# First mixer of a two-part transformer: chunk order, head grouping and attention placed among the weight chunks

## The chip, the core and the metric

The kernel runs as one program on one core of a Trainium2 chip. The metric is device microseconds for one execution, the median of several runs. TensorE (PE) multiplies matrices out of SBUF into the eight banks of PSUM; VectorE (DVE), ScalarE (ACT) and GpSimd (POOL) do the elementwise work; SyncE (SP) issues the weight loads.

## The reference

A sequence of 256 tokens with 1024 features passes through two two-layer models, all in f32. The order is: first mixer ("even"), convolutional feed-forward, forgetting attention ("fox"), convolutional feed-forward, gated feed-forward, recurrent mixer ("hgrn"), gated feed-forward, shared keys and values ("kv"), gated feed-forward, dilated attention, gated feed-forward. Each block works on a root-mean-square norm of the residual x and adds to it. Cut to the first mixer:

```
sq, sk, sv, nq, kc, vc, ksl, vsl, kwn, vwn, g = split_cols(h @ w_in, EVEN_SPLITS)
o_sb  = stick_breaking_attention(heads(sq), heads(sk), heads(sv))     # 8 heads of 64
o_nsa = nsa_attention(partial_rope(nq), kc, vc, partial_rope(ksl), vsl,
                      partial_rope(kwn), vwn, sigmoid(g), pos_k, pos_v, w_ck, w_cv)
return concat(o_sb, o_nsa) @ w_out
# stick breaking: z = q k / 8; log_keep = masked log_sigmoid(-z)
#   a = masked exp(log_sigmoid(z) + sum of log_keep over later keys);  o = a v
# nsa: kc, vc = windows of 32 tokens (every 16, 15 windows) + position, times w_ck, w_cv;
#   o = g0 * softmax over the 15 compressed + g1 * softmax over selected + g2 * softmax over window
```

With 256 tokens all selected blocks and the whole window are causal attention over everything, so the last two branches are ordinary causal softmaxes with their own keys and values: 8 heads x 2 branches, done as 8 units of two heads (4 pairs x 2 branches).

## The kernel before

x lies with features on partitions, as 8 tiles of 128 x 256. Before each block ScalarE writes xh, the f32r part of x times the gain (line 991), and VectorE writes xl, the remainder (line 891), by pairs of tiles; `act_prep` and `dve_prep` do this, with the squares for the norm, which is applied to results later. Weights come in chunks of 256 columns (1 MB) into a ring of three slots. ScalarE makes the high part of a chunk (line 342, `hi`) and VectorE or GpSimd the remainder (line 348, `lo`; the list `lo_by` says which). A product is three matmuls (lines 375 to 377), high by high, low by high, high by low; a chunk of both halves has 16 products of 256 columns, 48 matmuls. `chunk_mul` counts finished chunks: it frees a ring slot for the next high part, and `lo_ok` starts the next load. Each engine follows an order written out by hand; all coupling is by semaphores.

`make_even` holds the first mixer. TensorE (`pe_part`) takes chunks 0 to 11 in the order of the columns: queries and keys of the stick-breaking heads (0 to 3), their values (4, 5), queries of the other heads (6, 7), compressed keys and values (8), selected and windowed keys and values (9, 10, each with an extra half, 72 matmuls), gates (11, 24 columns). Only then come: the two position transposes, the compression (lines 1127 and 1132, 128 small matmuls) out of blocks that VectorE builds (line 1238); ten rotations (lines 1159, 1161) with VectorE's cosine and sine work (1251 to 1255); stick breaking for eight heads, namely scores (1145, 1146), suffix sums (1170 to 1174), values (1180, 1182), between them ScalarE's absolute value, exponential and logarithm (1326 to 1334) and VectorE's factors and masks (1259 to 1265); the compressed scores (1190), their softmax on VectorE and transposes (1197). Then the softmax stage (`Soft`, `soft_pe`, `soft_dve`, `soft_act`): scores (438), mask (531), maxima (536, 537), exponentials (604), reciprocals and gates (549, 551), weights (555), transposes (456 to 458), values (472 to 478), two rounds late. Last the four output chunks (`pe_residual`), whose activations are kept in xh and xl themselves, so that the next block's xh waits for the last chunk (`outputs_in_xh`).

The forgetting mixer uses the same softmax stage, but its chunks stand among the units by the hooks `before`, `mid`, `after` and `step`, and its outputs lie in `dk_r`.

## Time and profile before

| | us |
|---|---|
| median of 3 runs | 2120.63 (2119.83 to 2125.02) |
| profiled execution | 2131.83 |
| its span | 2130.0 |
| TensorE busy | 2002.0 (94%) |
| VectorE busy | 1239.2 (58%) |
| ScalarE busy | 993.7 (47%) |
| mean granted TensorE clock | 0.959 |

In the page's forty slices of 53 us, TensorE is at 9 or more in nearly all; the third and fourth slices have 8 and 7 busy tenths and a granted clock of 5 and 7 tenths. The chain that ended last lies to 79% on TensorE. Idle time counts only where it is on the engine that sets the end; the granted clock says how long a matmul takes while it is busy.

### The profile page before, as it was taken

What the parts mean: (1) busy time and instruction counts of PE and PEld (TensorE: products, weight loads), DVE (VectorE), ACT (ScalarE), POOL (GpSimd) and SP (SyncE); (2) the same over time, 40 slices, a digit from 0 to 9 for tenths busy, and PEclk for the clock granted to TensorE, in tenths of its full rate; (3) what the DMA queues carried; (4) which work ended last, traced back from release to release, by engine and by line L of the source; (5) the groups of instructions that cost most, each with busy time, mean ns of one, the idle gap of its engine ahead of it and who ended that gap; (6) DMA issues with size and microseconds to landing.
All of it is one profiled execution on the core that took longest, in us unless ns stands there. A gap on an engine that the chain in (4) does not pass through costs nothing.

```text
span 2130.0 us, 36855 instructions
## 1 busy us (share of the span) xinstructions
PE 2002.0 (94%) x15868; PEld 1913.7 (90%) x15868; DVE 1239.2 (58%) x1422; ACT 993.7 (47%) x1159; POOL 181.2 (9%) x74
## 2 busy tenths in 40 slices
PE   7887999999999989999886999999999998989999
PEld 7875899989899989999886999999899997769998
DVE  5327476675676676557785655543455565546554
ACT  4225444454544454346433533476743446655333
POOL 0100000001000000000341000033200010230000
PEclk9857899999999999999988999999999999999999
DMA  7300354444255435554321455545455545425552
GB/s 285 134 7 1 104 178 177 159 178 140 100 186 188 179 138 178 180 188 165 130 80 41 171 183 177 178 155 170 158 178 179 186 150 189 126 80 178 178 179 98
DMA packets 57569, 321.13 MB, mean 151 GB/s; under 512 B 5949, under 2 KB 19380, under 8 KB 20084
## 3 DMA queue, kind: packets, MB, share of 16 engines
q1 hardware_dynamic: 55700, 313.93, 42.6%
q10 hardware_dynamic: 1760, 5.63, 0.7%
q8 instruction: 84, 1.38, 0.3%
q14 instruction: 25, 0.20, 0.0%
HBM read 318.41 MB, written 1.12 MB: 150 GB/s over the span
## 4 chain that ended last, share of the span: by engine, by line
PE 79%; DVE 12%; ACT 5%; issue 2%; DMA 1%; SPq 0%; POOL 0%; ACTq 0%; DVEq 0%
PE bank L375 24%; PE bank L377 23%; PE bank L376 23%; DVE lo L348 3%; ACT hi L342 1%; DVE xl L891 1%; PE bank L438 1%; PE bank L475 1%; PE bank L1583 1%; DVE arena L531 1%; ACT arena L1744 1%; DVE arena L1658 1%; PE bank L1127 1%; PE bank L1132 1%; DVE x L904 1%
## 5 line engine op out<-in xcount | busy, mean ns | idle before, releaser
L375 PE MATMUL bank<-xh,hi 128*128 128x256 f32 x3080 | 885.1, 287 | 30.1 <-DVE xl L891 20.4
L376 PE MATMUL bank<-xl,hi 128*128 128x256 f32 x3080 | 878.3, 285 | 0.0
L377 PE MATMUL bank<-xh,lo 128*128 128x256 f32 x3080 | 877.9, 285 | 0.0
L348 DVE TENSOR_TENSOR lo<-ring,hi 128x2048 fp32r<-128x2048 f32 (+1 forms) x269 | 632.8, 2356 | 314.5 <-ACT hi L342 313.9
L342 ACT ACTIVATE hi<-ring 128x2048 fp32r<-128x2048 f32 x291 | 552.4, 1900 | 493.2 <-PE bank L377 486.3
L375 PEld LDWEIGHTS bank<-xh,hi 128*128 128x128 f32 x3080 | 597.5, 194 | 44.9 <-issue 31.2
L376 PEld LDWEIGHTS bank<-xl,hi 128*128 128x128 f32 x3080 | 597.6, 194 | 0.6 <-issue 0.5
L377 PEld LDWEIGHTS bank<-xh,lo 128*128 128x128 f32 x3080 | 597.4, 194 | 0.2
L375 PE MATMUL bank<-gh,hi 128*128 128x256 f32 x1056 | 300.1, 284 | 7.2 <-DVE gl L821 7.2
L376 PE MATMUL bank<-gl,hi 128*128 128x256 f32 x1056 | 299.4, 284 | 0.0
L377 PE MATMUL bank<-gh,lo 128*128 128x256 f32 x1056 | 299.3, 283 | 0.0
L375 PEld LDWEIGHTS bank<-gh,hi 128*128 128x128 f32 x1056 | 203.3, 193 | 8.2 <-DVE gl L821 8.2
L376 PEld LDWEIGHTS bank<-gl,hi 128*128 128x128 f32 x1056 | 203.4, 193 | 0.0
L377 PEld LDWEIGHTS bank<-gh,lo 128*128 128x128 f32 x1056 | 203.3, 193 | 0.0
L348 POOL TENSOR_TENSOR lo<-ring,hi 128x2048 fp32r<-128x2048 f32 (+1 forms) x22 | 97.7, 4439 | 1055.4 <-ACT hi L342 1055.4
L375 PE MATMUL bank<-hi,xh 128*128 128x256 f32 (+1 forms) x400 | 119.8, 300 | 0.9 <-DVE arena L1398 0.8
L376 PE MATMUL bank<-lo,xh 128*128 128x256 f32 (+1 forms) x400 | 114.5, 286 | 0.0
L377 PE MATMUL bank<-hi,xl 128*128 128x256 f32 (+1 forms) x400 | 114.4, 286 | 0.0
L852 ACT ACTIVATE gh<-arena 128x512 fp32r<-128x512 f32 x66 | 41.7, 632 | 126.1 <-DVE arena L818 126.1
L790 DVE TENSOR_TENSOR arena<-bank,rs_b 128x512 f32<-128x512 f32 x66 | 45.6, 691 | 94.0 <-PE bank L377 93.8
L531 DVE TENSOR_TENSOR arena<-bank,arena 128x384 f32<-128x384 f32 x80 | 40.8, 552 | 75.0 <-PE bank L458 35.9
L375 PEld LDWEIGHTS bank<-hi,xh 128*128 128x128 f32 x400 | 78.6, 197 | 4.2 <-issue 2.8
(268 smaller groups left out, 2002.8 us busy)
## 6 DMA issues: line engine op xcount, KB each, us to landing
ring<-in_ffn_in SPq DMA_DIRECT2D x132, 1024.0 KB, 4.9
ring<-in_ffn_out SPq DMA_DIRECT2D x66, 1024.0 KB, 4.9
ring<-in_kv SPq DMA_DIRECT2D x24, 1024.0 KB, 4.9
ring<-in_hg_in SPq DMA_DIRECT2D x16, 1024.0 KB, 4.9
ring<-in_od_in SPq DMA_DIRECT2D x12, 1024.0 KB, 5.0
ring<-in_dq SPq DMA_DIRECT2D x12, 1024.0 KB, 4.9
ring<-in_ev_in SPq DMA_DIRECT2D x11, 1024.0 KB, 5.7
arena<-rel_rows SPq DMA_DIRECT2D x24, 256.0 KB, 3.8
```

The costliest lines, as they stand in the source:

```text
L342: nc.scalar.activation(hi[n % RING][:, 0:words[n]], ring[n % RING][:, 0:words[n]], ACT.Copy).then_inc(hi_ok, 1)
L348: ns.tensor_tensor(lo[n % RING][:, 0:w], ring[n % RING][:, 0:w], hi[n % RING][:, 0:w].bitcast(F32), ALU.subtract).then_inc(lo_ok[lo_by[n]], 1)
L375: nc.tensor.matmul(out_, lh, rh, start=start, stop=False, **kw)
L376: nc.tensor.matmul(out_, lh, rl, start=False, stop=False, **kw)
L377: return nc.tensor.matmul(out_, ll, rh, start=False, stop=stop, **kw)
L438: last = nc.tensor.matmul(soft_bank(w, e)[:, c0:c1], sub["q"][:, q0:q0 + P], sub["k"][:, 0:k1], start=True, stop=one)
L475: nc.tensor.matmul(out[e][:, 0:T], un["subs"][e][g]["v"][0], s.pt[w % 2][e][:, 0:T], start=un["first"] and g == 0, stop=False, skip_group_ ...
L531: nc.vector.tensor_tensor(a[e][:, g, :], soft_bank(w, e)[:, 0:384], un["subs"][e][g]["add"], ALU.add).then_inc(soft_sem["masked"], 1)
L790: nc.vector.tensor_tensor(dst, ga, rs2, ALU.mult).then_inc(ff_read, 1)
L852: nc.scalar.activation(gh[:, par, :, :], ff_g[:, par, :, :], ACT.Copy).then_inc(gh_ok, 1)
L891: last = nc.vector.scalar_tensor_tensor(xl[:, t, :], x[:, t, :], gain_of(b, t), xh[:, t, :].bitcast(F32), ALU.mult, ALU.subtract)
L904: nc.vector.scalar_tensor_tensor(xs, y, scale, xs, ALU.mult, ALU.add).then_inc(x_new, 1)
```

## The change

- The first mixer's chunks come in the order stick-breaking queries, keys and values of the first four heads (0, 2, 4 of before), compressed keys and values (8), selected and windowed keys (9), their values (10), the other queries (6, 7), the gates, and then queries, keys and values of the last four stick-breaking heads (1, 3, 5). The columns of the weights are regrouped beforehand, so that keys of both branches share a chunk, as do the values, and no chunk has an extra half. The other heads are paired (0,4), (1,5), (2,6), (3,7), so that each pair's two heads belong to the two groups; the duplicating constants are gone.
- Stick breaking runs in two groups of four heads: the first among chunks 3 to 6, the second behind the softmax stage, among the output chunks.
- Rotation is applied to a raw copy of a whole chunk, 512 columns at once, three times; norm and scale are folded into the cosine and sine.
- Compression is one run of 32 matmuls with keys and values merged in the weights (128 columns) against blocks filled up with zeros.
- The softmax stage has six half chunks (9, 10, 11, all in bank 3) among its first six rounds, the compressed softmax spread over rounds 0 to 4, and the output chunks go by tiles in the order 0, 1, 4, 5, 6, 7, 2, 3.
- All remainders of the first mixer are made by VectorE.
- Outputs of the first mixer lie in `dk_r`. After "hgrn" and "kv" the last chunk's second half frees xh by pairs of tiles (`xh_free`), where the whole chunk was awaited.

```diff
-            "even": [cols("ev_in", CW * c) for c in range(11)] + [cols("ev_in", 2816, 24)]
+            "even": [cols("ev_in", CW * c) for c in (0, 2, 4, 8, 9, 10, 6, 7)] + [cols("ev_in", 2816, 24)]
+            + [cols("ev_in", CW * c) for c in (1, 3, 5)]
...
-            elif b == "hgrn":
+            elif b in ("even", "hgrn"):
...
+                if freed and h == 1 and k in (1, 3, 5):
+                    last.then_inc(xh_free, 1)
...
+                if i == 2 and outputs_in_xh(r):
+                    for t in range(3):
+                        low(t)
...
-            return r["kind"] == "add" and r["y"][0][0] == "c" and r["after"] not in ("fox", "dilated")
+            return r["kind"] == "add" and r["y"][0][0] == "c" and r["after"] not in ("even", "fox", "dilated")
...
+            by_tiles = r["kind"] == "regain" or outputs_in_xh(r)
+            if info[b]["c0"] > 0 and not by_tiles:
+                act.wait_ge(chunk_mul, info[b]["c0"] - 2)
             if b == plan[0]:
                 hi_until(act, 0)
             for i in range(4):
                 if r["kind"] != "regain":
                     act.wait_ge(x_new, r["x0"] + i + 1)
+                if by_tiles:
+                    act.wait_ge(*((xh_free, r["free0"] + i + 1) if i < 3 else (chunk_mul, info[b]["c0"])))
                 for e in range(2):
...
+            def sb_bank(grp, i):
+                return bank[4 * (1 - grp) + i]
...
+            rope_chunk, rot_bank = (4, 6, 7), (5, 4, 5)
+            rope_dst = (KD[:, :, :], NQ[:, 0:2, :], NQ[:, 2:4, :])
+            rope_scale = (1.0, DH ** -0.5, DH ** -0.5)
...
+            def pe_rot(pe, r):
+                pe.wait_ge(raw_ok, r + 1)
+                nc.tensor.matmul(bank[rot_bank[r]][:, :], C["rot"][:, :], RAW[:, r % 2, :, :], start=True,
+                                 stop=True).then_inc(rot_mm, 1)
...
+            def dve_cos(dve, r):
+                dve.wait_ge(raw_ok, r + 1)
+                nc.vector.scalar_tensor_tensor(rope_dst[r], halves(bank[rope_chunk[r] % 4]), rope_scale[r], two(COSR[:, :]),
+                                               ALU.mult, ALU.mult).then_inc(cos_ok, 1)
...
+            def dve_rope(dve, r):
+                dve.wait_ge(rot_mm, r + 1)
+                if r >= 1:
+                    dve.wait_ge(rope, r)
+                nc.vector.scalar_tensor_tensor(RT[:, :, :], halves(bank[rot_bank[r]]), rope_scale[r], two(SINR[:, :]),
+                                               ALU.mult, ALU.mult).then_inc(rope_t, 1)
+                dve.wait_ge(rope_t, r + 1)
+                dve.wait_ge(cos_ok, r + 1)
...
+            def pe_compress(pe):
+                pe.wait_ge(cmp_in, 16 * 2)
+                pe.wait_ge(blk_ok, 8)
+                for l in range(32):
+                    last = nc.tensor.matmul(bank[7][:, 0:64], CW_[:, l, :], BLOCKS[:, l, :], start=l == 0, stop=l == 31)
+                last.then_inc(comp, 1)
...
+            def out_part(pe, c, ks):
+                for h in range(2):
+                    if h == 0 and 0 in ks and c >= 2:
+                        pe.wait_ge(*soft.at("o", c + 1))
+                    pe_part_of(pe, n0 + 12 + c, bank[4 + c], h, ks, lambda k: pe.wait_ge(*of_tile(k)), (out_h, out_l),
+                               tile_order)
...
+            def pe_round_half(c, h):
+                def run(pe):
+                    if (c, h) == (9, 0):
+                        pe.wait_ge(cos_ok, 3)
+                    elif h == 0:
+                        pe.wait_ge(pj_fm, c - 6)
+                    pe_half(pe, n0 + c, bank[3], "tm" if c == 11 else "fm", h)
+                    if (c, h) == (9, 0):
+                        pe_cmp_scores(pe)
+                return run
...
+            soft.before["pe"] = {0: pe_first, 8: pe_last_scores}
+            soft.after["pe"] = {2: pe_turn_two, 3: pe_turn_third, 4: pe_turn_fourth}
+            soft.turn_after = {1: (c_pt, 2), 3: (c_pt, 4)}
...
+            soft.before["dve"] = {1: lambda dve: lo_until(dve, n0 + 11), 2: lambda dve: dve_evict(dve, 9),
+                                  4: lambda dve: dve_evict(dve, 10)}
+            soft.mid["dve"] = {0: dve_first}
+            soft.after["dve"] = {1: dve_cmp_weights, 3: lambda dve: lo_until(dve, n0 + 12),
+                                 5: lambda dve: lo_until(dve, n0 + 13), 7: lambda dve: lo_until(dve, n0 + 14)}
+            soft.tail["dve"] = {7: lambda dve: sb_keep(dve, 1)}
...
+            soft.mid["act"] = {1: act_cmp_exps, 3: act_pairs_turned, 4: lambda act: act_cmp_turned(act, 2),
+                               5: lambda act: act_cmp_turned(act, 3)}
+            soft.after["act"] = {2: lambda act: hi_until(act, n0 + 12), 4: lambda act: hi_until(act, n0 + 13),
+                                 6: act_last_values, 8: lambda act: sb_abs(act, 1), 9: lambda act: sb_logs(act, 1)}
...
+            def pe_part(pe):
+                pe_chunk(pe, n0, bank[0], "fm", first=first_xg("even"))
+                pe_stats(pe, "even")
+                pe_chunk(pe, n0 + 1, bank[1], "fm")
+                pe_chunk(pe, n0 + 2, bank[2], "tm")
+                pe.wait_ge(pos_in, 16 * 2)
+                nc.tensor.transpose(bank[6][:, 0:64], PE_[0:64, :], ident[0:64, 0:64]).then_inc(pos_t, 1)
+                pe.wait_ge(pj_fm, 2)
+                pe.wait_ge(pos_ok, 1)
+                sb_scores(pe, 0)
+                pe_chunk(pe, n0 + 3, bank[3], "fm")
+                pe.wait_ge(pj_fm, 1)
+                pe_chunk(pe, n0 + 4, bank[0], "fm")
+                pe.wait_ge(const_in, 16)
+                pe.wait_ge(ones_ok, 2)
+                sb_suffix(pe, 0)
+                pe.wait_ge(pj_fm, 2)
+                pe_chunk(pe, n0 + 5, bank[1], "tm")
+                pe.wait_ge(pj_tm, 1)
+                sb_values(pe, 0)
+                pe_rot(pe, 0)
+                pe_chunk(pe, n0 + 6, bank[2], "fm")
+                pe_compress(pe)
+                pe.wait_ge(pj_fm, 3)
+                pe_chunk(pe, n0 + 7, bank[3], "fm")
+                pe_compressed_keys(pe)
+                pe_rot(pe, 1)
+                pe.wait_ge(cos_ok, 1)
+                pe_chunk(pe, n0 + 8, bank[0], "tm", 24)
+                pe.wait_ge(rope, 1)
+                pe_rot(pe, 2)
+                soft_pe(pe, soft)
+                out_part(pe, 0, (0, 1, 4, 5))
+                out_part(pe, 1, (0, 1, 4, 5))
+                sb_suffix(pe, 1)
+                out_part(pe, 0, (6,))
+                out_part(pe, 1, (6,))
+                out_part(pe, 2, (0, 1, 4, 5))
+                sb_values(pe, 1)
+                for c in range(2):
+                    out_part(pe, c, (7,))
+                out_part(pe, 2, (6, 7))
+                for c in range(3):
+                    out_part(pe, c, (2, 3))
+                for h in range(2):
+                    pe_half(pe, n0 + 15, bank[7], "fm", h, acts=(out_h, out_l))
...
+            def dve_ahead(dve):
+                nc.vector.memset(BLOCKS[:, :, :], 0.0).then_inc(ones_ok, 1)
+                nc.vector.memset(ONES[:, :], 1.0).then_inc(ones_ok, 1)
...
+            def dve_part(dve):
+                lo_until(dve, n0 + 3)
+                dve_evict(dve, 0)
+                dve_evict(dve, 1)
+                lo_until(dve, n0 + 4)
+                dve.wait_ge(pos_t, 1)
+                nc.vector.tensor_copy(PEK[:, :, :], bank[6][:, 0:64].rearrange("p (i l) -> p i l", i=2)).then_inc(pos_ok, 1)
+                lo_until(dve, n0 + 5)
+                dve.wait_ge(const_in, 16)
+                for dst, n in ((COSR, "cos"), (SINR, "sin")):
+                    nc.vector.tensor_tensor(dst[:, :], C[n], rs_b[:, :], ALU.mult).then_inc(cs_ok, 1)
+                sb_keep(dve, 0)
+                dve_evict(dve, 3)
+                lo_until(dve, n0 + 6)
+                dve.wait_ge(cs_ok, 2)
+                dve_cos(dve, 0)
+                dve.wait_ge(ones_ok, 2)
+                dve.wait_ge(pos_ok, 1)
+                dve.wait_ge(pj_fm, 3)
+                sb_mask(dve, 0)
+                for i in range(2):
+                    for g in range(2):
+                        r = slice(g * DH, (g + 1) * DH)
+                        kv = KCV[r, i, :].rearrange("p (c l) -> p l c", l=16)
+                        for hf in range(2):
+                            pos = PEK[r, i, 16 * hf:16 * hf + 16].unsqueeze(2).broadcast_to([DH, 16, N_CMP])
+                            nc.vector.tensor_tensor(BLK[r, 16 * hf:16 * hf + 16, i, g, 0:N_CMP], kv[:, :, hf:hf + N_CMP], pos,
+                                                    ALU.add).then_inc(blk_ok, 1)
+                lo_until(dve, n0 + 7)
+                dve_rope(dve, 0)
+                sb_low(dve, 0)
+                lo_until(dve, n0 + 9)
+                dve_cos(dve, 1)
+                dve.wait_ge(comp, 1)
+                nc.vector.tensor_copy(KVR[:, :], bank[7][:, 0:64]).then_inc(kvr_ok, 1)
+                dve_cos(dve, 2)
+                dve_compressed_keys(dve)
+                dve_rope(dve, 1)
+                lo_until(dve, n0 + 10)
+                dve.wait_ge(pj_tm, 3)
                 soft_dve(dve, soft)
+                sb_mask(dve, 1)
+                sb_low(dve, 1)
+                lo_until(dve, n0 + 15)
...
             def act_part(act):
+                for i in range(2):
+                    act.dma_start(PE_[32 * i:32 * i + 32, :], A["cmp_pos"][:, i * P:(i + 1) * P]).then_inc(pos_in, 16)
...
+                act_evict(act, 2)
+                hi_until(act, n0 + 5)
+                sb_abs(act, 0)
+                sb_logs(act, 0)
+                hi_until(act, n0 + 6)
+                act_raw(act, 0)
+                hi_until(act, n0 + 7)
+                sb_exps(act, 0)
+                act_evict(act, 5)
+                hi_until(act, n0 + 8)
+                sb_high(act, 0)
+                act_raw(act, 1)
+                hi_until(act, n0 + 9)
+                act_raw(act, 2)
+                hi_until(act, n0 + 10)
+                act_evict(act, 8)
+                hi_until(act, n0 + 11)
                 soft_act(act, soft)
-            return {"pe": pe_part, "dve": dve_part, "act": act_part}
+                sb_exps(act, 1)
+                sb_high(act, 1)
+            return {"pe": pe_part, "dve": dve_part, "act": act_part, "dve_ahead": dve_ahead}
```

## Rows read from the trace of the kernel before

**Rows 1.** Stretches: length, busy (x) of PE, PEld, DVE, ACT, POOL; PEclk, DMA share, GB/s.
```profile
17.90:96.50 78.60, 78.59 (x631) 78.42 (x631) 34.38 (x31) 30.98 (x30) 9.85 (x3) 0.99 0.56 206
96.50:222.60 126.10, 99.55 (x642) 77.67 (x641) 61.94 (x177) 46.40 (x120) 4.56 (x1) 0.62 0.05 17
445.00:576.00 131.00, 126.85 (x1012) 114.10 (x1010) 76.63 (x139) 72.45 (x138) 18.67 (x4) 1.00 0.38 132
```

**Rows 2.** Waits between 96 and 223 us; columns: total, times, longest.
```profile
PE bank L1127 <- DVE arena L1238: 6.5, 1, 6.5
...
PE bank L1170 <- DVE arena L1262: 5.7, 1, 5.7
```

**Rows 3.** Busy time by stretch, pieces of the attention, columns as in rows 1.
```profile
103.50:130.40 26.90, 26.74 (x256) 26.44 (x256) 0.07 (x1) 0.00 (x0) 0.00 (x0) 0.50 0.12 40
151.20:154.30 3.10, 3.06 (x16) 2.68 (x16) 0.00 (x0) 1.03 (x3) 0.00 (x0) 0.50 0.00 0
164.50:168.90 4.40, 4.40 (x32) 4.13 (x30) 4.30 (x10) 1.01 (x3) 0.00 (x0) 1.00 0.00 0
169.00:172.60 3.60, 3.58 (x33) 2.52 (x32) 2.74 (x7) 3.48 (x9) 0.00 (x0) 1.00 0.00 0
```

**Rows 4.** Timeline of TensorE at three edges; columns: start, duration, instruction, idle before.
```profile
249.02 0.55 PE L375 MATMUL bank<-xh,hi 128*128 128x256 f32 x1 [2.01 <-DVE xl L891]
...
577.28 0.39 PE L375 MATMUL bank<-xh,hi 128*128 128x256 f32 x1 [0.96 <-DVE xl L891]
...
1538.33 0.35 PE L375 MATMUL bank<-xh,hi 128*128 128x256 f32 x1 [3.12 <-DVE xl L891]
```

**Rows 5.** Timeline of VectorE and ScalarE during the output chunks.
```profile
235.54 0.69 DVE L904 SCALAR_TENSOR_TENSOR x<-bank,x 128x512 f32<-128x512 f32 x1 [1.46 <-PE bank L377]
...
241.30 0.69 DVE L904 SCALAR_TENSOR_TENSOR x<-bank,x 128x512 f32<-128x512 f32 x1 [1.46 <-PE bank L377]
243.31 2.29 DVE L348 TENSOR_TENSOR lo<-ring,hi 128x2048 fp32r<-128x2048 f32 x1 [1.31 <-ACT hi L342]
...
241.36 1.92 ACT L342 ACTIVATE hi<-ring 128x2048 fp32r<-128x2048 f32 x1 [3.84 <-PE bank L377]
```

**Rows 6.** Timeline of TensorE, one softmax unit.
```profile
198.32 0.92 PE L438 MATMUL bank<-arena 64*128 64x256 f32 x8
...
200.26 0.65 PE L472 MATMUL bank<-arena 15*64 15x256 f32 x4
200.84 0.65 PE L475 MATMUL bank<-arena 128*64 128x256 f32 x4
...
201.64 0.49 PE L438 MATMUL bank<-arena 64*128 64x256 f32 x2
```

**Rows 7.** Groups of instructions by shape, VectorE; columns: busy, mean ns, idle before.
```profile
L1238 DVE TENSOR_TENSOR arena<-arena 128x240 f32<-128x240 f32 x4 | 6.2, 1610 | 0.0
```

**Rows 8.** Busy time by stretch, compressed softmax and softmax stage, columns as in rows 1.
```profile
173.50:185.00 11.50, 5.57 (x48) 4.11 (x48) 3.19 (x11) 2.21 (x5) 0.00 (x0) 0.67 0.00 0
185.00:199.00 14.00, 11.29 (x60) 8.22 (x60) 11.59 (x40) 8.79 (x34) 0.00 (x0) 0.54 0.00 1
199.00:213.00 14.00, 11.50 (x94) 6.92 (x90) 13.76 (x49) 10.96 (x41) 0.00 (x0) 1.00 0.00 1
```

**Rows 9.** Timeline of VectorE, one softmax round.
```profile
199.64 1.01 DVE L531 TENSOR_TENSOR arena<-bank,arena 128x384 f32<-128x384 f32 x2
...
201.61 0.17 DVE L549 RECIPROCAL arena<-arena 128x4 f32<-128x4 f32 x1
...
203.43 0.55 DVE L531 TENSOR_TENSOR arena<-bank,arena 128x384 f32<-128x384 f32 x1
```

**Rows 10.** Timeline of ScalarE, logarithms of the stick-breaking heads.
```profile
156.55 1.28 ACT L1334 ACT_TABLE_LOAD   x1
157.84 3.41 ACT L1334 ACTIVATE arena<-arena,one_c 128x768 f32<-128x768 f32 x4
```

**Rows 11.** Timeline of ScalarE after keys and values.
```profile
1536.37 2.89 ACT L991 ACTIVATE xh<-x,vecs 128x256 fp32r<-128x256 f32 x7
```

More of the change, by code:

```diff
@@ L662, in pe_stats, with pe_half @@
                                  stop=True).then_inc(fin_stat, 1)
-        def pe_half(pe, n, B, mode, h, width=CW, first=None, tiles=None, acts=None):
+        def pe_half(pe, n, B, mode, h, width=CW, first=None, tiles=None, acts=None, freed=False):
             if h == 0:
@@ L1193, in pe_part, with pe_cmp_turn @@
                 last.then_inc(c_qk, 1)
-                pe.wait_ge(c_p, 1)
-                for h in range(8):
+            def pe_cmp_turn(pe, p, B):
+                for e in range(2):
                     for t in range(2):
-                        last = nc.tensor.transpose(bank[h // 2][0:N_CMP, (h % 2) * T + t * P:(h % 2) * T + (t + 1) * P],
-                                                   CP[:, 8 * (h % 2) + 2 * (h // 2) + t, 0:N_CMP], ident[:, :])
+                        last = nc.tensor.transpose(B[0:N_CMP, e * T + t * P:e * T + (t + 1) * P],
+                                                   CP[:, 8 * e + 2 * p + t, 0:N_CMP], ident[:, :])
@@ new lines, in act_evict @@
+            def act_evict(act, c):
+                act.wait_ge(chunk_mul, n0 + c + 1)
+                B = bank[c % 4 if c < 9 else 3]
+                for t in range(2):
+                    y, r = B[:, t * CW:(t + 1) * CW], rs_c[:, t:t + 1]
+                    if c == 8:
+                        last = nc.scalar.activation(GT[:, t, :], y[:, 0:24], ACT.Sigmoid, scale=r)
+                    elif c == 5:
+                        last = nc.scalar.activation(VSW[:, :, t, :], y.rearrange("p (b d) -> p b d", b=2), ACT.Copy, scale=r)
+                    else:
+                        v = SV[:, t, 0:CW] if c == 2 else SV[:, t, CW:2 * CW]
+                        last = nc.scalar.activation(v, y, ACT.Copy, scale=r)
+                last.then_inc(pj_tm, 1)
```

501 lines of the change are left out of this document (233 added, 268 removed).

## The prediction

> **What bounds the kernel now.** I read the busy time and clock by stretches first, one to a block. TensorE is busy nearly all of every feed-forward block, so the place to look is the first mixer: its twelve input chunks are dense, and then come 126.1 us with 99.6 us busy at a mean granted clock of 0.62, which lies near the lower level (1.2 of 2.4 GHz) [rows 1]. The forgetting mixer, which weaves its attention between its chunks, fills 126.9 of 131.0 us at clock 1.00 [rows 1]. Next the waits in the bad stretch: TensorE waits 6.5 us for the compression's blocks, 5.7 us for the stick-breaking factors, and less for smaller things [rows 2]; that is too little to explain it. The cost is mostly work issued alone at half clock: compression alone is 26.9 us at 0.50 [rows 3]. So before, TensorE runs from 17.9 to 247.0 (the next block's first product starts at 249.02 after 2.01 idle [rows 4]): 229.1 us, all of it on the path that sets the end.
>
> **The dense work that is left.** Price everything on TensorE at the upper level.
> Input chunks: 78.6 us before [rows 1], the slow first one included. Chunks 9 and 10 lose a third of their 72 products each (the half computed in both orders). A chunk of 48 products takes 5.76, from 241.30 minus 235.54, when two of them were taken up [rows 5], so this is 48 x 0.12 = 5.8 less. Taking 78.4 up to the last product: 72.6.
> Stick-breaking: scores of 4 heads took 3.1 at clock 0.50 [rows 3], so 1.55 at the upper level, twice: 3.1. Suffix products of five heads 4.4 at 1.00, 0.88 a head: 7.0 for 8. Value products of 8 heads 3.6 [rows 3].
> Rotation: 16 products of 256 columns become 3 of 512; a 512-column head of the suffix takes 0.88: 2.6.
> Compression: 128 small products become 32 with 128 weight columns and 64 moving columns. The old row gives 26.9/128 = 0.21 at half clock [rows 3]. Below: half of that, 0.105 x 32 = 3.4. Above: each full-width weight load costs as much as a product of a chunk (0.12) and an f32 product appears as two instructions (256 for the old 128), so 0.24 x 32 = 7.7. I take 7.5, since the wider weights are new and the chunk row has just that width.
> Compressed keys 1.0 (six small products; 0 to 2); compressed scores 2.0 (16 of the small kind, 0.12 each); 16 transposes at (200.26 - 198.32 - 0.92)/6 = 0.17 each [rows 6], 2.7; positions 0.3.
> Eight softmax units: one with compressed values takes 201.64 - 198.32 = 3.32; without them 0.58 less [rows 6]: 4 x 3.32 + 4 x 2.74 = 24.2.
> Output: four chunks 23.0 and 0.3 for opening three banks.
> Sum: 72.6 + 3.1 + 7.0 + 3.6 + 2.6 + 7.5 + 1.0 + 2.0 + 2.7 + 0.3 + 24.2 + 23.3 = 149.9. Without any stall the block would end at 167.8.
>
> **Where it will still stall.** I walked the three instruction orders against each other.
> TensorE's row of work, with the durations above: chunks 0 to 2 until 38.6, scores, chunks 3 and 4, suffix products until 56.0, chunk 5 until 61.8, values and first rotation, chunk 6 until 70.2, compression, chunk 7, keys, second rotation, chunk 8 until 92.3, third rotation, and round 0 of the softmax stage from about 93. Until chunk 6 each wait is covered by a chunk. Eight block additions replace four, on half the partitions but with the same 240 elements each. The old ones take 1.61 us [rows 7]; below, half of it if only partitions counted; I take the full price, 12.9 us. VectorE reaches them at about 58.8, after the last stick-breaking mask, and ends at 71.7, where chunk 6 ends at 70.2: 1.5 us stall. Chunk 7's remainder is queued behind them, but compression covers it.
> The softmax stage may start when ScalarE has the gates of chunk 8: 0.7, with a table load ahead of it. In round 0 the compressed scores wait for the third rotation, which VectorE does after the first masks: 0.7.
> The largest one is round 2. Chunks 9, 10 and 11 share one bank, so chunk 10 waits for VectorE's eviction of chunk 9, and on VectorE ahead of it stand: the first part of the compressed softmax 1.4 (all of it is 3.2 busy, some 3.5 with gaps [rows 8]), the remainder of chunk 11 2.29 [rows 5], the masks of unit 1 (201.61 - 199.64 = 2.0), the weights of unit 0 (203.43 - 201.61 less 0.4 for a pair's low part: 1.4 to 1.5) [rows 9], the other part of the compressed softmax 2.1, the eviction 0.7. Starting at 99.5 that gives 109.5; TensorE is there at 105.3: 4.2 stall. Everything behind chunk 10 on TensorE, the first transposes too, is queued behind this wait. Chunk 11: 0.3.
> From round 6 no chunk is left to fill. VectorE needs 3.5 a round and 2.3 for a remainder in every second, TensorE 3.0: stalls of 0.3 in round 7 and 1.4 in round 9. The second stick-breaking group: ScalarE starts its exponential at 147.4 (1.48, a table load of 1.28, then logarithms of 0.9 each [rows 10]), VectorE's factors end at 155.4, while the first two output chunks cover TensorE to 154.6 and the suffix products to 158.1: nothing.
> Chunk 15 takes the ring slot of chunk 12, which is now finished almost last, at 168.5; its high and low parts take 1.9 + 2.3 [rows 5] and the hand-over: 172.8, where TensorE would be at 171.4: 1.4 stall. Waits for the transposed positions at the start: 0.6.
> Together 11.1: the block ends at 179.0 instead of 247.0, 68 us less. I take off 2 for a lower clock in rounds 7 to 9 and 2 for hand-overs between engines that a walk on paper leaves out.
> Side costs I set to nothing: the clearing of the blocks stands before VectorE's first copy, while it waits for the load of the vectors (bounds 0 to 1). The remainders that GpSimd made go to VectorE, counted above. ScalarE gets three more table loads of 1.28 [rows 10], 3.8 us in all. Their cover is the waits for chunks; without it 1.3 each is on the path, at most in the gates and in the second group.
> On those loads the Trainium skill (ScalarE: Activation LUTs, Table sets: the hidden batching unit) gives some 2.7 us a load; the trace has 1.28 and decides, by the page the second group would come 1.4 later, and be covered too.
>
> **The edges between blocks.** First mixer to feed-forward: outputs no longer lie in the normed input, so this edge becomes like the one after the forgetting mixer, 0.96 instead of 2.01 [rows 4], with a small second wait behind it: 0.6. Recurrent mixer: pairs 0 to 2 are ready early, but the third low part now stands ahead of the last residual on VectorE, and the last pair waits 1.4 behind the start: 0.5 gained (bounds -0.5 to 2.0). Shared keys and values to the next block: 3.12 idle [rows 4], and freeing by pairs buys nothing, since ScalarE starts the normed input at 1536.37 with no idle time before it [rows 11], 1.2 after the last product, straight behind other work of its own, and so is itself late (bounds 0 to 2). Together 1.1.
>
> **The sum.** 68 - 2 - 2 + 1.1 = 65 us off. The profiled execution took 2131.8 us (span 2130.0), 11.2 above the median of 2120.6; the gain is taken as the same in both: 2067 profiled, 2056 for the median.
>
> **Rivals.**
> *Denser than I think.* If VectorE's pieces overlap as in the woven mixer, and chunk 10 doesn't wait, the block ends at 167.8: 79 + 1 off, 2040. For it: the forgetting mixer idles only 4 of 131 us [rows 1]. Against: it has twelve chunks to put between eight units, this one three.
> *The attention pieces keep the lower clock.* The unwoven softmax ran at 0.54 in one stretch and at 1.00 in the next [rows 8]. Were rounds 6 to 9 and the compression at the lower level, this costs 12 - 4 = 8 (rounds of which 4 is hidden in VectorE's time) and 7.5: 15 more, 2071. Against: a chunk half stands next to most pieces. The Trainium skill (TensorE: Matmul & The Clock Gate, Part 4: PE-mode transpose) says that transposes don't count as activity for the clock in the same way, which speaks for this case; the stretch at 1.00 held transposes in every round, which speaks against.
> *Slower than before.* One mechanism: the short gaps after chunk 2 drop the clock and the mixed work never brings it back until the block ends. Of the dense work 149.9 - 20.7 = 129 us comes later than chunk 2; at half clock it costs 129 more, 2185. It is slower than before from the point where 65 of these 129 us run at the lower level. In the stretch before, 126 us averaged 0.62, so it isn't impossible; the woven mixer's 1.00 speaks against.
> *It doesn't do what it says* holds for the keys-and-values edge, where I expect no gain; it is in the sum.
>
> **How the numbers follow.** Forecast 0.51, denser 0.17, lower clock 0.28, slower 0.04. The forecast alone spans 2046 to 2066 (each stall from nothing to double). The range 2040 to 2079 takes in most of both neighbours, the compression's lower price and the late ScalarE. Under 0.3%, 6.4 us, can't be told from no change; between the cases that fall there I put 0.01. Faster 0.95, same 0.01, slower 0.04.
>
> **What would show it.** The output chunks' last product near 182, not 247; compression as one run of some 7.5 us; clock at 0.95 or more from chunk 2 to the outputs; an idle gap of some 4 us ahead of chunk 10 released by VectorE's eviction; VectorE's 1.61 us additions eight times; the idle before the block after keys and values still near 3.1. I am wrong if TensorE waits on VectorE in most rounds, if the clock sits at 0.5 in the softmax stage, or if the end comes from another block.

## The result and the profile after

| us | before | after |
|---|---|---|
| median, same rounds | 2122.82 (2119.83 to 2130.67, 4 runs) | 2067.28 (2065.64 to 2069.61, 4 runs) |
| profiled execution | 2131.83 | 2066.73 |
| its span | 2130.0 | 2064.9 |
| mean granted clock | 0.959 | 0.979 |

The ratio is 0.9734, 95% interval 0.9704 to 0.9763: faster. The profiled executions lie 65.1 us apart, as forecast (65); the medians lie 55.5 apart, so the forecast of the median, 2056, is 11 too low.

Where it went, by stretches of the profile after (length, busy of PE, PEld, DVE, ACT, POOL, then PEclk, DMA share, GB/s):

```profile
16.90:82.00 65.10, 64.66 (x525) 62.60 (x526) 41.41 (x54) 33.77 (x40) 0.00 (x0) 1.00 0.54 196
82.00:95.00 13.00, 13.00 (x64) 10.86 (x63) 4.96 (x10) 6.22 (x6) 0.00 (x0) 0.61 0.24 82
95.00:109.40 14.40, 9.27 (x95) 8.46 (x93) 11.99 (x33) 4.13 (x17) 0.00 (x0) 0.97 0.22 73
109.40:115.00 5.60, 5.60 (x26) 5.60 (x27) 3.33 (x12) 0.00 (x0) 0.00 (x0) 0.50 0.01 3
115.00:151.60 36.60, 33.11 (x273) 24.74 (x271) 27.12 (x73) 29.44 (x82) 0.00 (x0) 1.00 0.27 87
151.60:183.60 32.00, 30.45 (x241) 28.44 (x240) 16.60 (x23) 15.21 (x20) 0.00 (x0) 1.00 0.17 56
379.50:510.50 131.00, 126.83 (x1010) 113.78 (x1010) 76.35 (x142) 72.24 (x138) 18.69 (x4) 1.00 0.38 135
```

The first mixer now ends at 183.6 (forecast: 183.0) where it ended at 247.0 [rows 1], and the 126 us at 0.62 are gone. What is left of the lower level (1.2 GHz) stands in the second and fourth rows. The forgetting mixer (last row) is what it was. TensorE's five largest waits, 17 to 190 us (total, times, longest):

```profile
PE bank L374 <- DVE xl L895: 6.8, 3, 5.3
PE bank L374 <- DVE arena L1319: 5.0, 2, 4.6
PE bank L457 <- DVE arena L556: 2.7, 3, 1.2
PE bank L374 <- DVE lo L347: 1.5, 1, 1.5
PE bank L1111 <- DVE arena L1473: 0.4, 1, 0.4
```

The 5.3 us of the first row are the kernel's start; L1319 is the eviction (VectorE's copy of a finished chunk out of its PSUM bank) that chunk 10 waits for. The wait for the compression's blocks [rows 2] is gone. In the last row, the first scores wait 0.4 for the transposed positions. The first products behind the waits, and the four edges between blocks; start, duration, instruction, idle before:

```profile
109.40 0.58 PE L374 MATMUL bank<-xh,hi 128*128 128x256 f32 x1 [4.64 <-DVE arena L1319]
...
176.96 0.39 PE L374 MATMUL bank<-dk_r,hi 128*128 128x256 f32 x1 [1.55 <-DVE lo L347]
...
184.74 0.39 PE L374 MATMUL bank<-xh,hi 128*128 128x256 f32 x1 [1.11 <-DVE xl L895]
...
186.13 0.39 PE L374 MATMUL bank<-xh,hi 128*128 128x256 f32 x1 [0.41 <-DVE xl L895]
...
513.52 0.39 PE L374 MATMUL bank<-xh,hi 128*128 128x256 f32 x1 [1.25 <-DVE xl L895]
...
1121.88 0.38 PE L374 MATMUL bank<-xh,hi 128*128 128x256 f32 x1 [1.48 <-DVE xl L895]
...
1472.49 0.36 PE L374 MATMUL bank<-xh,hi 128*128 128x256 f32 x1 [3.11 <-DVE xl L895]
```

Against [rows 4] the next block starts 64.3 us earlier, so practically the whole gain is made here. Compression and block additions, by shape (busy, mean ns, idle before):

```profile
L1222 PE MATMUL bank<-arena 128*128 128x64 f32 x64 | 7.3, 274 | 0.0
```

```profile
L1493 DVE TENSOR_TENSOR arena<-arena 64x240 f32<-64x240 f32 x8 | 4.2, 569 | 0.1
```

Compression cost 7.3 where 7.5 was forecast and 26.9 stood before [rows 3]. An addition costs 0.57, not the 1.61 of [rows 7].

### The profile page after: what moved, and what is told of

It reads as the page before. It is cut to its first block, busy times and chain, and to the rows that moved or that the text cites. A ratio compares the mean times of both kernels' runs of the same rounds, so it can differ in the third digit from the quotient of the medians.

```text
span 2064.9 us, 36350 instructions
## 1 busy us (share of the span) xinstructions
PE 1953.2 (95%) x15614; PEld 1871.3 (91%) x15614; DVE 1240.4 (60%) x1409; ACT 996.6 (48%) x1163; POOL 167.2 (8%) x70
## 4 chain that ended last, share of the span: by engine, by line
PE 79%; DVE 12%; ACT 6%; issue 2%; DMA 1%; SPq 0%; POOL 0%; ACTq 0%; DVEq 0%
PE bank L374 24%; PE bank L376 24%; PE bank L375 24%; DVE lo L347 4%; ACT hi L341 2%; DVE xl L895 1%; PE bank L439 1%; DVE x L908 1%; PE bank L476 1%; ACT arena L1936 1%; PE bank L1775 1%; DVE arena L1850 1%; DVE arena L532 0%; PE bank L457 0%; DVE arena L1857 0%
## 5 line engine op out<-in xcount | busy, mean ns | idle before, releaser
L374 PE MATMUL bank<-xh,hi 128*128 128x256 f32 (+1 forms) x3016 | 867.0, 287 | 34.1 <-DVE xl L895 19.7
L375 PE MATMUL bank<-xl,hi 128*128 128x256 f32 (+1 forms) x3016 | 859.1, 285 | 0.0
L376 PE MATMUL bank<-xh,lo 128*128 128x256 f32 (+1 forms) x3016 | 858.7, 285 | 0.0
L347 DVE TENSOR_TENSOR lo<-ring,hi 128x2048 fp32r<-128x2048 f32 x273 | 640.1, 2348 | 311.0 <-ACT hi L341 310.1
L374 PEld LDWEIGHTS bank<-xh,hi 128*128 128x128 f32 (+1 forms) x3016 | 583.8, 194 | 49.7 <-issue 26.6
L375 PEld LDWEIGHTS bank<-xl,hi 128*128 128x128 f32 (+1 forms) x3016 | 584.1, 194 | 0.8 <-issue 0.7
L376 PEld LDWEIGHTS bank<-xh,lo 128*128 128x128 f32 (+1 forms) x3016 | 583.9, 194 | 0.2
L347 POOL TENSOR_TENSOR lo<-ring,hi 128x2048 fp32r<-128x2048 f32 x18 | 83.3, 4627 | 1005.1 <-ACT hi L341 1005.1
```

The lines of the kernel that those rows point to most:

```text
L347: ns.tensor_tensor(lo[n % RING][:, 0:w], ring[n % RING][:, 0:w], hi[n % RING][:, 0:w].bitcast(F32), ALU.subtract).then_inc(lo_ok[lo_by[n]], 1)
L374: nc.tensor.matmul(out_, lh, rh, start=start, stop=False, **kw)
L375: nc.tensor.matmul(out_, lh, rl, start=False, stop=False, **kw)
L376: return nc.tensor.matmul(out_, ll, rh, start=False, stop=stop, **kw)
```

## The experiments

The kernel before was run beside all ten, the changed kernel only in the first measurement. Kernels derived from the changed one are therefore set against its 2067.28 and its trace; of medians of different rounds I use no difference under 2 us. The second yardstick is the trace: the start of the next block's first product, 184.74 us in the changed kernel. The two disagree by up to 3 us, so that a difference of that size needs a reason in the rows:

| against the changed kernel, us | median | next block's start |
|---|---|---|
| four remainders on GpSimd | -1.5 | +0.6 |
| compression in small pieces | +17.9 | +18.2 |
| eviction of chunk 9 earlier | -6.9 | -3.9 |
| gates turned round | -8.8 | -7.2 |
| both, and chunk 12 first | -13.2 | -12.0 |
| attention not among the chunks | +4.6 | +4.9 |
| second group ahead | +4.0 | +5.0 |
| freeing as a whole | 0.0 | +2.2 |

**The kernel before again.** No edit.

> The kernel before, unchanged, run again to price the term by which the forecast of the median missed (the profiled execution of before took 2131.83 us against a median of 2120.63; the changed kernel 2066.73 against 2067.28). Theory 1 (before scatters from execution to execution, because its bare attention stretch sits where the granted clock falls or not): five rounds spread by over 5 us, the profiled execution lies anywhere between 2118 and 2134, and its span less that of the first profiled execution (2130.0) is found in the stretch 96.5:222.6, whose mean clock was .62. Rival 2 (the profile itself costs this kernel some 10 us): the new profiled execution lies 8 to 13 us above the median again. Rival 3 (one chip differs from another): profile and rounds agree within 3 us and both lie elsewhere than 2120.6.

Median 2121.07 of 12 runs, 2115.23 to 2131.37; profiled 2127.67. Over all rounds of this study the kernel before has 56 runs, 2115.2 to 2132.5, median 2122.7. Runs at a mean clock of .966 or more took at most 2120, runs at .959 at least 2126. So theory 1 holds as to the scatter, and the first profiled execution lay at its top. Rival 2 isn't excluded here (the new profile is 6.6 above its median), but in the next experiment the profile lies 5.0 below. The place was only in part the one that theory 1 named (96.5 to 222.6). Up to the last softmax wait both profiles take 115.3 us; they part in TensorE's work from there to the end of the output chunks, the same 236 to 238 records (first the execution of the forecast, then the new one):

```profile
212.90:247.00 34.10, 33.28 (x236) 28.74 (x236) 12.51 (x19) 9.68 (x15) 0.00 (x0) 0.85 0.20 65
```

```profile
211.80:241.60 29.80, 28.69 (x238) 26.18 (x236) 12.84 (x21) 9.94 (x17) 0.00 (x0) 1.00 0.24 76
```

The first execution fell to the lower level once more, behind a softmax wait of 1.90 us, and stayed there for ten; the new one waited 1.11 and did not fall:

```profile
215.00:225.00 10.00, 10.00 (x49) 6.11 (x46) 1.56 (x5) 2.08 (x5) 0.00 (x0) 0.50 0.00 1
```

The stretch is 4.3 us longer for it. The wait alone doesn't decide it: in the next experiment's profile the same wait is again 1.90, and the clock behind it 1.00. This shows one place; that the rest of the scatter arises likewise is argued from the clocks of the runs.

**No remainder on GpSimd, kernel before.**

```
-            elif b == "hgrn":
+            elif b in ("even", "hgrn"):      # VectorE makes them
```

> The kernel before with the remainders of the first block's input product all made by VectorE, as in the changed kernel; GpSimd makes none of them. Theory 1 (the mean of 1.61 us of the block additions at L1238, of which the fastest took .55 and the slowest 4.75 us, is one addition that ran beside a remainder on GpSimd): all four additions take .55 to .60 us, the wait of TensorE for them (6.5 us) falls to 2 to 3, and the kernel is about 4 us faster. Rival 2 (the additions are dear by themselves, by their strided output): one of them still takes over 2 us and the time stays within 1 us. Rival 3 (VectorE is short of time here, so that four more remainders of about 1.5 us each delay the additions by as much as GpSimd's did): additions of .57 us, wait of 5 us or more, time the same or up to 3 us slower.

2120.23 (12 runs), ratio to before 0.9994 (0.9975 to 1.0014): the same. First, what stood behind the mean of 1.61: all four additions of the kernel before (min/median/max), and GpSimd's remainder beside them:

```profile
L1238 DVE TENSOR_TENSOR arena<-arena x4: 552/569/4752, 97.4 to 98.8; 128x240 f32<-128x240 f32 x4
```

```profile
98.67 4.56 POOL L348 TENSOR_TENSOR lo<-ring,hi 128x2048 fp32r<-128x2048 f32 x1 [24.12 <-ACT hi L342]
```

Three took some 0.57; the fourth, started at 98.8 beside GpSimd's, took 4.75 and ended 0.3 behind it (103.2). Then the new kernel, waits of TensorE and the additions:

```profile
PE bank L1120 <- DVE arena L1231: 4.5, 1, 4.5
PE bank L1127 <- DVE arena L1238: 2.3, 1, 2.3
```

```profile
L1238 DVE TENSOR_TENSOR arena<-arena 128x240 f32<-128x240 f32 x4 | 1.9, 548 | 0.0
```

Theory 1 is right on the additions (0.55) and wrong on the time: the remainder now makes VectorE late for the copy ahead of them (L1231), so that TensorE waits 4.5 + 2.3 instead of 0.3 + 6.5. In substance that is rival 3. This profile's span is 12.4 shorter than the one before it (2113.4 to 2125.8): 7.8 of that lie in the first mixer, 4.6 behind it, where nothing was edited, so the scatter isn't all in this mixer.

**Four remainders back to GpSimd, changed kernel.**

```
-            elif b in ("even", "hgrn"):
+            elif b == "hgrn":
```

> The changed kernel with every third remainder of the first block's input product (chunks 5, 8, 11, 14) made by GpSimd again; nothing else. Theory 1 (VectorE and GpSimd slow each other): the VectorE instruction that lies beside GpSimd's remainder of about 4.6 us is stretched to up to 4.6 us; chunk 11 is delayed or the eviction of chunk 9 comes later, 1 to 4 us slower, and with the remainder of chunk 14 off VectorE the stall of 1.55 us before chunk 15 shrinks to under .5. Rival 2 (GpSimd is idle anyway, so its remainders only relieve VectorE, which is late for chunks 10 and 15): no VectorE instruction is stretched, 1 to 4 us faster.

2065.76 (2064.66 to 2066.97): 1.5 less, not a difference that I use, and in the trace the next block starts 0.6 later. Each theory names something that happens, in different rounds. Chunk 11's remainder on GpSimd relieves VectorE: the wait before chunk 10 is 2.81 instead of 4.64. Chunk 14's does this (VectorE and GpSimd):

```profile
136.92 4.52 POOL L347 TENSOR_TENSOR lo<-ring,hi 128x2048 fp32r<-128x2048 f32 x1 [39.85 <-ACT hi L341]
```

```profile
137.62 0.41 DVE L537 TENSOR_REDUCE arena<-arena 128x1 f32<-128x256 f32 x1
...
138.83 2.63 DVE L552 TENSOR_TENSOR arena<-arena 128x4 f32<-128x4 f32 x1
141.50 1.16 DVE L556 TENSOR_TENSOR arena<-arena 128x256 f32<-128x256 f32 x4
142.58 0.17 DVE L550 RECIPROCAL arena<-arena 128x4 f32<-128x4 f32 x1
142.78 0.17 DVE L552 TENSOR_TENSOR arena<-arena 128x4 f32<-128x4 f32 x1
```

A product of 4 elements a partition takes 2.63 us beside GpSimd and 0.17 without it, while the reduction at 137.62 isn't stretched; TensorE waits 3.3 in that round. Behind this wait the clock is at the lower level for ten us, where the changed kernel had 1.00, and that uses up the relief before chunk 10:

```profile
143.00:153.00 10.00, 10.00 (x47) 5.36 (x46) 2.31 (x7) 7.81 (x14) 0.00 (x0) 0.50 0.24 94
```

The wait before chunk 15 stayed at 1.55.

**Compression in small pieces, changed kernel.**

```
-                for l in range(32):
-                    last = matmul(bank[7][:, 0:64], CW_[:, l, :], BLOCKS[:, l, :])
+                for g in range(2):
+                    for i in range(2):        # 64x64 weights, 15 columns
+                        for l in range(32):
+                            last = matmul(bank[7][o, ...], CW_[r, l, o], BLK[r, l, i, g, 0:N_CMP])
```

> The changed kernel with the compression as 128 matmuls of 64x64 weights against 15 columns in place of the 32 of 128x128 against 64; one wait of TensorE on itself at half way orders the two row groups, some .2 us. Theory 1 (a small matmul costs the same fixed pace as in the kernel before, where 128 took about 13.6 us by .106 each): the compression takes 13 to 14.5 us in place of 7.3, and the kernel is 6 to 7 us slower. Rival 2 (128 small ones against 32 large ones is even: the pace is set by the columns and the weight rows): 7 to 9 us, at most 1.5 us slower. Rival 3 (small matmuls make the chip lower the clock, as in the kernel before): the granted clock falls to .5 in the compression and chunk 7 behind it takes about 4 to 6 us more, 10 us or more slower in all.

2085.13 (2083.71 to 2089.42), 17.9 slower. Stretches (the first two are compression, the third mostly chunk 7, the fourth chunk 8 and what follows, the last stands behind the wait before chunk 10):

```profile
67.70:71.00 3.30, 3.30 (x55) 3.30 (x56) 0.85 (x1) 2.40 (x2) 0.00 (x0) 0.95 0.24 97
71.00:92.00 21.00, 20.94 (x204) 20.80 (x203) 2.04 (x2) 0.00 (x0) 0.00 (x0) 0.50 0.15 51
92.00:105.00 13.00, 13.00 (x88) 12.26 (x87) 3.93 (x9) 3.68 (x3) 0.00 (x0) 0.76 0.00 1
105.00:114.00 9.00, 9.00 (x36) 7.10 (x37) 1.51 (x3) 3.53 (x4) 0.00 (x0) 0.50 0.35 117
128.70:131.00 2.30, 2.29 (x10) 2.29 (x11) 2.23 (x9) 0.00 (x0) 0.00 (x0) 0.50 0.00 0
```

Rival 3 is right: the small products start at the upper level and fall to half of it with TensorE busy without a break (20.94 of 21.0). Compression takes 24.3 instead of 7.3. At its opening pace (55 records in 3.3 us, 256 in all) it would take 15.4, so about 8 of the 17 are the larger number and 9 the clock. (The expectation's 13.6 for 128 is no time of the kernel before, which took 26.9 at the lower level [rows 3]; it is about half of that, the price at the upper level.) Chunk 7 stays at the lower level to about 98 and loses some 3, not 4 to 6. So merging removed more than issues: half of what it is worth is the clock.

**Eviction of chunk 9 earlier, changed kernel.**

```
-  before["dve"] = {1: lo_until(n0 + 11), 2: dve_evict(9), 4: dve_evict(10)}
-  after["dve"]  = {1: dve_cmp_weights, 3: ...}
+  before["dve"] = {4: dve_evict(10)}
+  after["dve"]  = {1: dve_evict(9) + dve_cmp_weights, 2: lo_until(n0 + 11), 3: ...}
```

> The changed kernel with VectorE's list in the softmax stage reordered: the eviction of chunk 9 goes ahead of the compressed weights, and the remainder of chunk 11 goes behind round 2. It aims at the stall of 4.64 us before chunk 10 and at the half clock in which the first half of chunk 10 then ran (5.5 us where 2.9 would do). Theory 1 (the stall is the order of VectorE's list, and the clock fell because of the stall): stall under 2 us, chunk 10 at full clock, 4 to 6 us faster. Rival 2 (the stall goes, the clock falls all the same): 2 to 3.5 us faster. Rival 3 (the late remainder of chunk 11 holds TensorE before chunk 11 by what was gained): within 1 us.

2060.35 (2059.60 to 2061.96), 6.9 faster; by the traces the output chunks end 3.9 earlier. The waits for evictions, the stretch of chunk 10, and a part of chunk 11:

```profile
PE bank L374 <- DVE arena L1319: 2.8, 2, 1.9
```

```profile
105.10:111.00 5.90, 5.90 (x49) 5.43 (x50) 5.66 (x20) 2.40 (x3) 0.00 (x0) 1.00 0.01 3
119.50:122.80 3.30, 3.30 (x17) 3.30 (x17) 2.82 (x11) 0.00 (x0) 0.00 (x0) 0.50 0.79 290
```

Before chunk 10 TensorE waits 0.85, and the chunk runs at 1.00: theory 1, at this place the clock fell with the wait. But part of the loss has moved, as rival 3 had it: before chunk 11 TensorE now waits 1.91 instead of 0.40, and behind that the clock is at 0.50 for 3.3 us. By the rows, 3.8 of wait and 2.8 of clock (half of 5.6) are gained at chunk 10, and 1.5 of wait and some 1.7 of clock given back at chunk 11: an estimate of 3.4 for the 3.9 of the trace. The 3 us more of the medians have no row.

**Gates turned round, changed kernel.**

```
-  pe_chunk(pe, n0 + 8, bank[0], "tm", 24)
+  pe_chunk(pe, n0 + 8, bank[0], "fm", 24)     # 24 x 256 result, turned back by two transposes
```

> The changed kernel with the gates' chunk (24 columns) turned round: the 24 weights' columns are held and 256 tokens stream, 48 matmuls of 256 columns in place of 96 of 24, and the gates are turned back by two transposes. In the changed kernel it took 8.7 us and the granted clock fell to .50 in it, for it, the third rotation and round 0's scores. Theory 1 (matmuls of few columns cost a fixed pace and let the clock fall, as the small compression showed, whose clock fell to .50 some 3.5 us after its start): the chunk takes 5.1 to 5.5 us, the clock stays at 1.00 from 80 to 95, rotation and scores take half, 5 to 8 us faster. Rival 2 (the clock falls by time and not by what is streamed): the chunk takes over 7 us, at most 2 us faster. Rival 3 (TensorE is ahead of VectorE here, so that what it gains becomes a longer wait before chunk 10): 0 to 2 us faster, the stall of 4.64 us grows by what was gained.

2058.50 (2057.05 to 2063.27), 8.8 faster; by the traces the output chunks end 7.2 earlier. The expectation's counts are wrong: the trace has 48 matmuls of 24 columns in the changed kernel and 24 of 256 here, so the edit halves their number too. The chunk takes 3.2 us (82.55 to 85.78) instead of 8.5 (82.02 to 90.55); the 48 at the pace that they had before the clock fell, one every 0.11, would be some 5.4, so that about 2 of the 5.3 are the number and 3 the clock (estimates). Stretches: chunk 8 with what surrounds it, then the wait before chunk 10 (4.64, unchanged), then chunk 10:

```profile
80.00:95.00 15.00, 14.40 (x131) 11.80 (x130) 9.60 (x22) 9.26 (x15) 0.00 (x0) 1.00 0.22 71
95.00:103.20 8.20, 3.30 (x28) 2.86 (x27) 7.96 (x22) 2.27 (x9) 0.00 (x0) 1.00 0.35 128
103.20:109.00 5.80, 5.73 (x36) 5.65 (x37) 3.41 (x13) 0.73 (x2) 0.00 (x0) 0.71 0.00 0
```

Theory 1 again: with 256 columns the clock stays, and behind the unchanged wait it falls, though for some 3.4 us and not 5.6. Rival 3 is out, since the stall didn't grow. (In the small compression the clock fell 3.0 us after its start, not the expectation's 3.5.)

**Both, and chunk 12's output first.**

```
+                out_part(pe, 0, (2, 3))        # chunk 12 whole, before the others
-                for c in range(3):
+                for c in (1, 2):
```

> Both edits together, and the output product begins with the whole of chunk 12's part, so that the buffer that chunk 15 waits for (1.55 us) comes free earlier. Theory 1 (the three losses are separate): 10 to 14 us faster than the changed kernel, about 2054 to 2057. Rival 2 (VectorE bounds the softmax stage, so that a faster TensorE only waits for it): 3 to 7 us faster. Rival 3 (as 2, and the longer waits let the clock fall elsewhere): within 2 us of the changed kernel.

2054.06 (2052.27 to 2056.56), ratio to before 0.9689 (0.9669 to 0.9710); 13.2 faster than the changed kernel and the fastest here. The losses are separate: 3.9 + 7.2 + 1.55 is 12.7, and the output chunks end at 171.6, 12.0 earlier. TensorE's three largest waits, 80 to 180 us:

```profile
PE bank L374 <- DVE arena L1320: 2.8, 2, 1.9
PE bank L457 <- DVE arena L556: 2.7, 3, 1.2
PE bank L374 <- DVE xl L895: 1.5, 2, 1.1
```

Behind the 1.92 us before chunk 11 (in the first row) the clock is again 0.50, from 112.4 to 115.7: the next some 3 us to be had.

**Attention not among the chunks.** Chunks 9 to 11 ahead of the softmax stage; the rounds follow bare.

```
+                for c in (9, 10, 11):
+                    for h in range(2): pe_round_half(c, h)(pe)
-  soft.step = {(2 * i + h, 0): pe_round_half(9 + i, h) ...}
+  soft.step = {(0, 0): pe_cmp_scores}
```

> The changed kernel with the selected attention not among the chunks: chunks 9 to 11 run whole ahead of the softmax stage, and its rounds follow bare. The forecast counted on the chunks filling TensorE's time between the rounds. Theory 1 (weaving fills the waits and keeps the clock): the bare rounds 0 to 9 leave the waits of the kernel before (TensorE busy about .6 to .7, clock falling to .5 in part), 12 to 25 us slower. Rival 2 (VectorE and ScalarE bound the softmax stage by some 60 us whether chunks lie in it or not, so that the 15 us of chunks are hidden there and come on top here): 8 to 12 us slower, clock 1.00. Rival 3 (the woven order loses as much by its stall before chunk 10 as it fills): within 3 us.

2071.91 (2071.35 to 2073.09), 4.6 slower: between the cases. The bare stage is bound by VectorE, busy 35.60 of 38.50, and loses clock:

```profile
117.50:156.00 38.50, 28.27 (x206) 18.49 (x206) 35.60 (x106) 31.90 (x94) 0.00 (x0) 0.87 0.23 79
```

It gives back the 4.64 before chunk 10 and its half clock, which is why the loss is so small: the weaving as it stands is worth 5 us, and 9 (by the traces) to 11 (by the medians) once chunk 9's eviction is early.

**The second group ahead of the output chunks.**

```
+                sb_suffix(pe, 1)
+                sb_values(pe, 1)
                 # output chunks 12 to 14 (the two calls stood among them)
```

> The changed kernel with the suffix sums and values of the second stick-breaking group ahead of the output chunks instead of between them. Theory 1 (the output chunks cover the chain exp, logs, suffix, keep, values of the second group): TensorE, done with the softmax stage at 151.6, idles until the logs and their split of 157.9 (6.3 us) and again between suffix sums and values (up to 4.7 us), less the 1.55 us before chunk 15, which vanish: 9 to 11 us slower. Rival 2 (the idle lets the clock fall as the stall of 4.64 us did, and the suffix sums and an output chunk run at half): 13 to 17 us slower. Rival 3 (without the chunks the chain itself starts earlier): under 5 us slower.

2071.31 (2069.97 to 2071.89), 4.0 slower: rival 3's size, for another reason. The one long wait, and the suffix products behind it:

```profile
PE bank L1119 <- DVE arena L1142: 3.2, 1, 3.2
```

```profile
154.10:159.70 5.60, 5.59 (x26) 4.90 (x26) 4.86 (x10) 2.62 (x4) 0.00 (x0) 0.70 0.00 0
```

TensorE can start when the first of four pieces is split (154.1), not the last, and the values follow without a gap. 3.2 idle and 2.1 for the lower clock (5.5 us instead of 3.4) is the price without cover; the 1.55 before chunk 15 didn't go.

**Freeing as a whole, and the old order of remainders at the edges.**

```
-  act.wait_ge(*((xh_free, r["free0"] + i + 1) if i < 3 else (chunk_mul, info[b]["c0"])))
+  act.wait_ge(chunk_mul, info[b]["c0"])
...                                 # and VectorE's low parts 0 to 2 behind the last residual again
```

> The changed kernel with the next block's input freed as a whole and the remainders of its normed input in the old order, at every edge between blocks. The forecast gave the edit by pairs 1.1 us: .6 at the end of the first mixer, .5 behind the gated recurrence, nothing behind the block of keys and values; the three gaps were then 1.5, 1.48 and 3.11 us where they had been 2.01, 2.01 and 3.12. Theory 1 (as forecast): the gaps go back to 2.0, 2.0 and 3.1, and the kernel is about 1 us slower, at the edge of what the rounds can tell. Rival 2 (the gap at the first edge has become shorter by the new chunk order and not by the pairs): it stays at 1.5, .5 us slower. Rival 3 (a transfer or the first block's start depends on the pairs too): 2 us slower or more.

2067.31 (2063.25 to 2069.32), no difference in the medians. The edges behind the first, the recurrent and the keys-and-values mixer:

```profile
186.98 0.39 PE L374 MATMUL bank<-xh,hi 128*128 128x256 f32 x1 [1.11 <-DVE xl L895]
...
1122.36 0.36 PE L374 MATMUL bank<-xh,hi 128*128 128x256 f32 x1 [2.07 <-DVE xl L895]
...
1475.29 0.36 PE L374 MATMUL bank<-xh,hi 128*128 128x256 f32 x1 [3.12 <-DVE xl L895]
```

Only the recurrent edge moves (1.48 to 2.07). The first one's gain doesn't come from the pairs; that it comes from outputs that no longer lie in the normed input, as the forecast's step said, is what is left, and no run tests it. The first mixer itself ends 2.2 later in this profile, though the edit leaves it alone: the clock was at 0.50 from 100.5 to 104, with no wait of over 0.5 in the 17 us before, and 0.54 from 148 to 152, where the changed kernel's was 1.00. So one trace of the new kernel, too, has 2 us of luck in it.

## Why the prediction was right, and where it wasn't

The profiled execution came out at 2066.73 for a forecast 2067, the first mixer's end at 183.6 for 183.0. Not every term was right:

- *The median.* "The gain is taken as the same in both" failed. It cost 11 us and put 2067.28 outside the forecast's own 2046 to 2066, though inside the range. The gain in the medians was 55.5, 9.5 less; the other 2 are the median of before, 2120.63 in the forecast's 3 runs and 2122.7 in 56. The profiled execution stood 11 above its median; 4.3 of that are found in a second fall of the clock in the very stretch that the change removes, the rest is argued from the clocks of the runs. After the change profile and median agree within 0.6. The new time should have been worked out by itself (2067, as its terms are priced at the upper level), and not as a difference taken off another, luckier run.
- *Block additions*, 12.9 us and 1.5 stall: wrong. 1.61 was the mean of three at 0.57 and one that GpSimd had held up; the changed kernel has no remainder on GpSimd in this block, and eight took 8 x 0.569 = 4.6 (the forecast's lower bound was 6.4). The minimum and maximum of the group would have shown it. The Trainium skill (SBUF — State Buffer, Who interferes with whom) says that VectorE and GpSimd share a pair of ports as an exclusive lock, and that a VectorE instruction with two SBUF inputs contends there with a GpSimd instruction that reads SBUF. The 4.75 and 2.63 us above agree; by it the term would have been estimated at 8 x 0.57 = 4.6 and the stall at nothing.
- *Stalls*: chunk 10's was forecast from 105.3 to 109.5 and measured 104.76 to 109.40; chunk 11 0.3 and 0.40; chunk 15 1.4 and 1.55; late rounds 1.7 and 2.7. The sum of 11.1 came out at 10.6 (length less busy time of the first six rows above).
- *Clock*, the term of TensorE's sum that was mis-sized most: 2 us taken off, in rounds 7 to 9. There the clock was 1.00. It was at 0.50 from 85.0 to 94.2 and from 109.4 to 115.0; half of 14.8 is 7.4 lost. The gates' chunk was in the dense sum with what it took before, 5.6 us (90.7 to 96.3, mean clock 0.92); here it took 8.5. That chunk with what follows it, and what stands behind chunk 10's wait, not the late rounds, were the place to look. What offset the 5.4 too little: hand-overs (2) that didn't show, stalls 0.5 shorter, a block that began at 16.94 instead of 17.9, and some 1 us less dense work. So the exact hit is in part cancelling errors.
- *Compression* 7.5: right (7.3).
- *Edges*: 0.5 for 0.6, 0.53 for 0.5, nothing for nothing. The edge after the forgetting mixer, untouched in the forecast, waits 1.25 instead of 0.96.
- *Rivals.* Denser didn't happen, since chunk 10 waits. The rival of the lower clock named compression and late rounds; neither kept it, but 7.4 us of its mechanism were there elsewhere. Compression in small pieces shows what a case of its size looks like.

## What to carry to other kernels

Forecast the new kernel's time from its own terms when the stretch removed is one whose clock varies; a difference against one profiled run carries that run's luck along. Read minimum and maximum of a group before its mean enters a sum, and look at what GpSimd did beside a stretched VectorE instruction. Price a merged or turned matmul at both levels of the clock: here the clock was half of what merging was worth (9 of 17 us). When one wait is removed, look at the next one on the same engine before counting the gain: of 6.6 us gained at chunk 10, 3.2 came back at chunk 11.

## What the runs showed of the hardware that I had not expected

- The clock fell with TensorE busy: from 0.95 to 0.50 in a run of 15-column products (20.94 of 21.0 us busy), and to 0.50 in the 24-column gates' chunk of the changed kernel, while the same chunk turned round ran at 1.00. Where in that chunk it fell differs: 2.6 us after its start in the changed kernel, 4.0 with the freeing as a whole.
- The length of a wait didn't settle the clock behind it. Waits of 4.64 us (changed kernel, small compression, second group ahead, gates turned), 3.5 (freeing as a whole), 3.3 (remainders on GpSimd) and 3.2 (second group ahead, before the suffix products) were followed by 0.50, and so were 1.91 and 1.92 (early eviction; both edits) and one of 1.90 in the kernel before. Behind 2.81 (remainders on GpSimd), 0.85 (early eviction) and the same 1.90 in the kernel before without remainders on GpSimd it was 1.00.
- A product of 4 elements a partition on VectorE took 2.63 us, and an addition of 240 a partition 4.75, each until GpSimd's instruction had ended; beside it neither reductions (0.41 and 0.27 us) nor a product that reads PSUM (0.68) were stretched.
